# TensorE takes the second expert row of each four in the value stage instead of the fourth, and the last tile's sum, norm and store are done in two halves

## The reference

```
idx  = top 16 of 8 heads per token            (128 expert indices a token)
a    = einsum('nhkd,nd->nhk', u_tab[idx], h)
coef = gate * gelu(a)
out  = einsum('nhk,nhkd->nd', coef, v_tab[idx])
x    = x + out
y    = rmsnorm(x, norm_final_g)
```

## Time and profile before

| | us |
|---|---|
| median of 3 runs | 4600.92 (4599.92 to 4604.53) |
| the profiled execution's own time | 4607.52 |
| its span in the trace | 4605.4 |

### The profile page before, as it was taken

The page is one execution under the profiler, slowest core; times in us unless marked ns, Lnnn a source line. Parts: engine busy times, 40 slices in busy tenths (PEclk is TensorE's granted clock), DMA queues, the critical chain, the costliest instruction groups (busy, mean ns, idle before and its releaser), DMA issues.

```text
span 4605.4 us, 61271 instructions
## 1 busy us (share of the span) xinstructions
PE 4106.5 (89%) x23624; PEld 3569.6 (78%) x23624; DVE 3098.9 (67%) x4558; ACT 918.3 (20%) x1338; POOL 1325.1 (29%) x822
## 2 busy tenths in 40 slices
PE   7999999999899989998898899999999998687555
PEld 7999999999789977887686778887778887353221
DVE  7434344435657568887487885888879657798766
ACT  4334434324333421021000000000000004000100
POOL 0000000000000023344251342444445431567664
PEclk9999999999899999999898999999999999787777
DMA  6555678775355569999798999999999997999998
GB/s 221 195 203 196 213 280 293 274 260 190 128 210 212 204 262 422 422 401 407 314 422 334 394 423 422 408 423 423 423 403 397 423 404 261 408 405 400 422 421 356
DMA packets 303268, 1529.06 MB, mean 332 GB/s; under 512 B 36394, under 2 KB 108538, under 8 KB 134948
## 3 DMA queue, kind: packets, MB, share of 16 engines
q0 software_dynamic: 114288, 830.54, 43.7%
q1 hardware_dynamic: 188772, 695.78, 39.9%
HBM read 1450.06 MB, written 76.13 MB: 331 GB/s over the span
## 4 chain that ended last, share of the span: by engine, by line
PE 54%; DMA 26%; DVE 8%; issue 5%; DVEq 3%; POOL 2%; ACT 2%; SPq 0%; ACTq 0%; POOLq 0%
PE psum L584 26%; PE psum L3329 10%; DMA sb_ring<-in_peer_v,sb_idx_all 10%; PE psum L650 10%; DMA sb_raw_u<-in_wstream 9%; DMA sb_raw<-in_wstream 5%; POOL sb_ring L3143 2%; PE psum L3585 2%; DVE sb_acc_b L3486 2%; DVE sb_acc L3169 1%; PE psum L3567 1%; DVE sb_split L568 1%; DVEq L2364 1%; DMA sb_ring<-in_peer_u,sb_idx_all 1%; DVE sb_ring L3164 1%
## 5 line engine op out<-in xcount | busy, mean ns | idle before, releaser
L584 PE MATMUL psum<-sb_actr,sb_split 128*128 128x264 f32 x7344 | 913.5, 286 | 29.2 <-DVE sb_split L568 17.3
L584 PEld LDWEIGHTS psum<-sb_actr,sb_split 128*128 128x128 f32 x7344 | 903.4, 190 | 33.8 <-issue 22.2
L568 DVE TENSOR_TENSOR sb_split<-sb_raw,sb_split 128x2048 fp32r<-128x2048 f32 x201 | 460.4, 2291 | 627.4 <-ACT sb_split L564 626.9
L3054 POOL DMA_INDIRECT sb_ring<-in_peer_u,sb_idx_all x256 | 419.5, 1639 | 1097.2 <-PE psum L584 522.4
L3169 DVE SCALAR_TENSOR_TENSOR sb_acc<-sb_ring,sb_coef,sb_acc 128x2048 f32<-128x2048 f32 x256 | 601.8, 2351 | 141.5 <-DMA sb_ring<-in_peer_v,sb_idx_all 127.3
L3164 DVE CUSTOM_DVE_ANT_0 sb_ring<-sb_ring,sb_htok 128x2048 f32<-128x2048 f32 x264 | 595.2, 2289 | 137.6 <-DMA sb_ring<-in_peer_u,sb_idx_all 132.2
L3054 POOL DMA_INDIRECT sb_ring<-in_peer_v,sb_idx_all x256 | 440.3, 1720 | 670.4 <-DVE sb_acc L3169 581.4
L3585 PE MATMUL psum<-sb_ring,sb_diag 128*128 128x512 f32 x512 | 350.0, 847 | 238.5 <-DMA sb_ring<-in_peer_v,sb_idx_all 232.6
L3486 DVE SCALAR_TENSOR_TENSOR sb_acc_b<-sb_ring,sb_coef_b,sb_acc_b 128x2048 f32<-128x2048 f32 x192 | 451.3, 2351 | 133.0 <-DMA sb_ring<-in_peer_v,sb_idx_all 120.0
L3143 POOL DMA_INDIRECT sb_ring<-in_peer_v,sb_idx_all x256 | 433.4, 1693 | 269.7 <-DVE sb_acc_b L3486 144.7
L3585 PEld LDWEIGHTS psum<-sb_ring,sb_diag 128*128 128x128 f32 x512 | 134.4, 276 | 438.1 <-DMA sb_ring<-in_peer_v,sb_idx_all 266.7
(11 more groups left out here) (451 smaller groups left out, 4484.3 us busy)
## 6 DMA issues: line engine op xcount, KB each, us to landing
sb_raw<-in_wstream SPq DMA_DIRECT2D x398, 1024.0 KB, 7.3
sb_raw_u<-in_wstream SPq DMA_DIRECT2D x64, 1024.0 KB, 22.3
sb_states<-in_state SPq DMA_DIRECT2D x32, 512.0 KB, 3.6
sb_states_t<-in_stateT SPq DMA_DIRECT2D x32, 512.0 KB, 4.3
out_gla_s<-sb_states SPq DMA_DIRECT2D x32, 512.0 KB, 3.0
dram_z<-sb_zst SPq DMA_DIRECT2D x121, 132.0 KB, 3.7
dram_z_b<-sb_zst SPq DMA_DIRECT2D x65, 128.0 KB, 1.8
sb_vrow<-dram_v SPq DMA_DIRECT2D x8, 1024.0 KB, 5.4
```

The lines of the kernel that those rows point to most:

```text
L568: nc.vector.tensor_tensor(split[:, slot, 1, :], raw[:, slot, :], split[:, slot, 0, :], ALU.subtract).then_inc(lo_ready, 1)
L584: last = nc.tensor.matmul(psum[:, bank, 0:ntok], w[a], acts(b, kt), start=(i == 0 and a == 0 and b == 0), stop=(i == len(kts) - 1 and a == 1))
L3054: nc.gpsimd.indirect_dma_start(ring[g % RING][:], None, ins[table], bass.IndirectOffsetOnAxis(ap=col, axis=0)) \
```

## The change

The choice of TensorE's rows moves from n % 4 = 3 to n % 4 = 1. The last tile's sum, square, scaling and store are each cut into two instructions over 1024 of the 2048 features; the sums of squares of the halves are added by a new small VectorE instruction.

```
+PE_AT_SLOT = 1
...
         def on_pe(n):
-            return n % PE_EACH == PE_EACH - 1
+            return n % PE_EACH == PE_AT_SLOT
...
-            return (...) if on_pe(n) else (SLOTS - SLOTS // PE_EACH) * y + n - n // PE_EACH
+            return (...) if on_pe(n) else (SLOTS - SLOTS // PE_EACH) * y + n - (n + PE_EACH - 1 - PE_AT_SLOT) // PE_EACH
...
# sp_last
-            store_y(sp, 4, acc_b[1], P)
-            sp.wait_ge(y_stored, 80)
+            for u, half in enumerate(HALVES):
+                sp.wait_ge(y_ready, 5 + u)
+                sp.dma_start(outs["y_prompt"][3 * P:4 * P, half], acc_b[1][:, half]).then_inc(y_stored, 16)
+            sp.wait_ge(y_stored, 96)
...
# act_last
-            act.wait_ge(acc_ready, 6)
-            act_norm(act, 4, acc_b[1], P)
+            for u, half in enumerate(HALVES):
+                act.wait_ge(acc_ready, 6 + u)
+                nc.scalar.activation(squares[:, half], acc_b[1][:, half], ACT.Square,
+                                     accum_out=small[:, 4 * u:4 * u + 1]).then_inc(squares_ready, 1)
+            act.wait_ge(root_in, ROOTS_Y + 5)
+            nc.scalar.activation(small[:, 2:3], small[:, 1:2], ACT.Sqrt).then_inc(root_out, 1)
...
# act_diags
-                n = PE_EACH * k + PE_EACH - 1
+                n = PE_EACH * k + PE_AT_SLOT
...
# dve_last
-            add_pe(dve, 1)
+            dve.wait_ge(row_used_pe, SLOTS // PE_EACH * 2)
+            dve.drain()
+            for half in HALVES:
+                nc.vector.tensor_tensor(acc_b[1][:, half].rearrange("p (b f) -> p b f", b=2),
+                                        psum[:, half.start // 512:half.stop // 512, :],
+                                        acc_b[1][:, half].rearrange("p (b f) -> p b f", b=2), ALU.add)
+                tile_done(dve)
+            dve.wait_ge(squares_ready, SQUARES_Y + 6)
+            nc.vector.tensor_tensor(small[:, 0:1], small[:, 0:1], small[:, 4:5], ALU.add)
+            dve.drain()
             norm_first(dve, 4, P)
-            norm_second(dve, 4, acc_b[1], P)
+            dve.wait_ge(root_out, ROOTS_Y + 5)
+            nc.vector.reciprocal(small[:, 3:4], small[:, 2:3])
+            dve.drain()
+            for half in HALVES:
+                nc.vector.scalar_tensor_tensor(out=acc_b[1][:, half], in0=acc_b[1][:, half], scalar=small[:, 3:4],
+                                               in1=gfin[:, half], op0=ALU.mult, op1=ALU.mult).then_inc(y_ready, 1)
```

More of the change, by code:

```diff
@@ L3360, in sp_last @@
             store_y(sp, 3, acc_b[0], P)
-            store_y(sp, 4, acc_b[1], P)
-            sp.wait_ge(y_stored, 80)
+            for u, half in enumerate(HALVES):
+                sp.wait_ge(y_ready, 5 + u)
+                sp.dma_start(outs["y_prompt"][3 * P:4 * P, half], acc_b[1][:, half]).then_inc(y_stored, 16)
+            sp.wait_ge(y_stored, 96)
+        HALVES = (slice(0, D // 2), slice(D // 2, D))
         def store_y(sp, q, src, rows):
```

2 lines of the change are left out of this document (1 added, 1 removed).

## The result

The changed kernel takes 4615.42 us (median of 10 runs, 4599.97 to 4620.49), the kernel before 4604.63 (10 runs, 4596.01 to 4608.29) beside it. The ratio is 1.0022, 95% interval 1.0013 to 1.0031: slower by 0.22%, where I forecast 4.5 us less. The profiled execution took 4618.24 us, its span is 4616.2.

What follows compares the result with a forecast made beforehand. DMA landings bound the value stage, leaving only the tail open. Tail -5.45 and boundary +1.0 make -4.45 us off the median 4600.92: 4596.5 us (chance 0.60); cases lie between 4593.7 and 4602.9, the range reaching up to 4602.

Steps and rivals of the forecast that it cites:

- The tail: From the last row's landing to the span's end: 12.69 us instead of 18.14, so 5.45 us less.
- The boundary: Between tiles, TensorE's first row waits for tile 0's add, delaying the gather of n = 9; 1.0 us lost, bounds 0 to 7.4.
- the rival of the catching-up gathers: After the tile boundary, POOL's gathers each wait behind a VectorE row; 1.3 us more, 4597.8 us; chance 0.07.
- The picks: Tile 0, where rows and picks share TensorE: the pattern only shifts by 6 slots, rows inside the same; put at nothing.
- the norms behind double slots cost their length: Tile 0: norm scalings right behind slots shared by TensorE's row and a pick add 4.7 us, 4601.2 us; chance 0.11.
- The argument against that rival: In the picks, VectorE's lateness can be used up at the next shared slot, where it waits for TensorE anyway.
- The 6.26 us stall at the first pick: POOL's wait before a gather at tile 0's first pick disappears, gaining up to 1.8 us; 4593.7 us with boundary hidden; chance 0.14.
- the rival on the slower side: At the tile boundary the queue hides nothing of n = 9's late gather; 1.95 us slower, 4602.9 us; chance 0.06.
- That TensorE's last row decides the end: In the tail, the last add waits for TensorE's row n = 125; some 1 us lost, 4597.5 us; chance 0.02.
- The gather at 4278.05: At the tile boundary, POOL's gather was read as taking 0.94 us while VectorE adds from PSUM.

Runs made afterwards that it cites:

- e5: The changed kernel once more, unaltered; 4609.19 us, 1.0016 of the kernel before.
- e6: Changed kernel with TensorE's one-hot matmuls issued four times in the pick ahead of each slot shared by row and pick, except the last; 4603.34 us, ratio 0.9992.
- e10: Changed kernel with tile 0's add done behind slot 0 of tile 1 instead of slot 2; 4613.15 us in one run.
- e11: e6 with tile 0's add also done behind slot 0 of tile 1 instead of slot 2; 4600.51 us, ratio 0.9991 to the kernel before.
- e2: Changed kernel with the first tile's three norms moved 6 slots later; 4607.59 us, ratio 1.0003 to the kernel before.
- e12: Kernel before (TensorE at slot 3) with the tail in halves and repeated one-hot matmuls ahead of shared row-and-pick slots, except the first; 4600.86 us, ratio 0.9986.
- e7: Changed kernel with the first tile's three norms moved into tile 1; 4609.19 us, ratio 1.0010 to the kernel before.
- e14: The same kernel as e7, run again; 4612.52 us in one run.
- e4: Kernel before with the first tile's three norms moved 6 slots earlier; 4610.29 us, ratio 1.0015 to the kernel before.
- e8: e7 with TensorE's rows at slot 3 instead of slot 1; 4608.82 us, ratio 1.0013 to the kernel before.

## Why the prediction was wrong

- **The tail: right.** Forecast 12.69 us, measured 12.8 in all ten profiles with slot 1. Half adds 1.23 (forecast 1.215), the last square 1.16 with its sum (1.15), the new sum 0.16, scalings 1.28. TensorE's last row was ahead of VectorE's with 2.06 us to spare where I had 0.9, because it took 5.23 us and not 6.38.
- **The boundary: mechanism right, the size too small.** I forecast that TensorE starts its first row at once behind the add and 7.4 us late, and that "0.6 to 1.4 us are lost; I take 1.0". Measured 2.5 (3.0 in e5 and e6), and e10 and e11 take it all back. The gather of n = 9 left at 4299.27, where it left at 4278.05 before, 21.2 us later, while the last row of tile 0 had started 13.5 us later (4279.4 against 4265.9): 7.7 us late, where I had 6.6 to 7.4. Of these 7.7 the queue hid 5.2, where I had 6.0. The term was mis-sized by 1.5 us; the bounds, 0 to 7.4, held it. The lone gather of n = 9 hid more than I had granted it (it landed in 5.7 us, I had 6.7); what I had left out are the 1.6 us at n = 10 and 11. That is the place, and about the size, of the rival of the catching-up gathers (1.3 us). But its rule of 2.81 us from gather to gather did not come: six gathers left within 8.5 us, 1.24 to 2.48 apart. That the two slow gather instructions are what cost the 1.6 us is argued from the order of events; no run separates it from the empty queue.
- **The picks: the step that failed.** "The rows inside are the same, so I put nothing." Rows and picks repeat after 12 slots and do come out the same shifted by 6, but the norms stand at fixed slots and do not shift. There were three patterns, and I carried over two of them. e2 shows it: with the norms shifted too, the last pick is at 315.6 us, as before at 315.8. And "the rows inside are the same" took their length as given: TensorE's double rows lasted 5.1 to 6.7 us, all eight, where four of them had lasted 3.6 to 3.7, and e6, with the norms left where they are, gives back 13.3 us by bringing them back to 3.6 to 3.7 in six of them.
- **The rival "the norms behind double slots cost their length": the right place, another mechanism, less than half the size.** It had 4.7 us and a chance of 0.11; measured is +10.9. It counted two scalings of the three (n = 22 and 58, not 48, which in the trace also comes behind its double slot, at 4069.74), but three lengths, 7.05 us, would not have been it either. With the clock up at six or seven double rows, norms in the changed kernel's place (e6, e11: 12 and 15 us lost), norms in the old place (e12: 12) and no norms (e7: 14) can't be told apart. With none up, the norms in the changed place cost about 3 us (24 to 28 against 23 in e14). The low clock at the double rows takes more: 9 us for six of them without norms (23 against 14 in e14 and e7), so some 6 for the four that this change lost. Together that is 9 of the 10.9, an estimate; no profile has the old place with all rows down, and the split isn't shown.
- **The argument against that rival fell.** It was that VectorE's lateness can be used up at the next double slot, where it waits for TensorE anyway. But a late VectorE holds its buffers, POOL sits (8.55 us), the next row lands late, TensorE idles (6.07 us) and meets the next row at the lower clock: the lateness is renewed and not used up. This chain is read from one stretch of the trace; e6, which breaks it at the clock, is what supports it.
- **The other rivals.** The 6.26 us stall at the first pick is gone (POOL's waits there are 3.7 us at most), but a gain from it can't be seen in any total. The queue hid most of the late gather, so the rival on the slower side, which had the boundary for its mechanism, fell; slower came by another way. That TensorE's last row decides the end did not happen.
- **A reading that was wrong.** The gather at 4278.05 was not one "while VectorE adds from PSUM": the add ended at 4278.09, and most of the gather's 0.94 us lay beside the next row. What told the short gathers from the long ones was which instruction had begun first, as the last section says. No term of the sum hung on it.

By the measured terms -5.4 + 2.5 + 10.9 = +8.0 us in the profile, against my -4.45, and in the two timings +10.8 (medians; 1.0022) and +4.2 (medians; the ratio of 1.0016 makes it 7.4). The base was low besides: I took the median of 3 runs, 4600.92, and that of 10 is 4604.63.

**Open.** What puts TensorE's clock down at one double row and not at another isn't settled: after an idle time of 1.35 to 1.36 us one row of the changed kernel took 5.70 us and another 3.70, and e7 and e14 show that it differs between executions. That the norms' places sway it is shown by e2 and e4, that it can also come without norms by e14 and e8; how it starts is not shown.

## What to carry to other kernels

When a pattern is shifted against another, list everything that stands at fixed slots, and not only the two that the change names; where three loops of work interleave, a long single piece (here a norm's scaling of 2.35 us) right behind the slot where they meet is worth moving once as a test. Where an engine's instruction waits on a landing and others wait on it, look at the granted clock in that very instruction: after idle time ahead of it the same work took up to 1.85 times as long here (6.67 against 3.60 us), and cheap matmuls into the wait can bring it back. When work is moved out of a stage, count its transfers as well as its instructions. And judge such an edit by several executions, with the time from a fixed point of its own stage.
